# A hybrid decoder step on one core: index queries projected first, index scores as two-head row tiles between the gated pieces, convolution taps in three stages

## The reference

```python
z = einsum('btd,de->bte', rms_norm(x), w_in)
q, k, v, gate_a, qi, ki, wi, glu_a, glu_b, gate_c = split(z)
u = glu_a * sigmoid(glu_b)
# index scores, 8 heads of 64
s = einsum('thd,ld->thl', qi, ki) * 64**-0.5
score = einsum('th,thl->tl', wi * 8**-0.5, relu(s))        # causal
idx = top_k(score, 256)
attn = softmax(q.k[idx] * 64**-0.5 + rel_bias) . v[idx]    # q and k are RMS-normed by head
# convolution branch
c = silu(layer_norm(causal_depthwise_conv(u, width 31) + dw_b))
y = x + concat(attn * silu(gate_a), c * silu(gate_c)) @ w_out
```

## Time and profile before

| | us |
|---|---|
| median of 3 runs (1035.41 to 1056.24) | 1039.91 |
| profiled execution | 1040.58 |
| its span, first to last instruction | 1038.8 |
| PE busy | 930.8 (90%) |
| DVE busy | 694.0 (67%) |
| ACT busy | 372.5 (36%) |
| POOL busy | 85.4 (8%) |

### The profile page before, as it was taken

How to read it: one execution, slowest core, us unless ns; L and a number is a source line. 1 busy time by engine, 2 the same in 40 slices (tenths; PEclk the granted TensorE clock), 3 DMA queues, 4 the chain that set the end, 5 groups by cost and what they waited for, 6 DMA issues and landing times.

```text
span 1038.8 us, 11317 instructions
## 1 busy us (share of the span) xinstructions
PE 930.8 (90%) x3900; PEld 514.4 (50%) x3900; DVE 694.0 (67%) x1598; ACT 372.5 (36%) x830; POOL 85.4 (8%) x90
## 2 busy tenths in 40 slices
PE   3999999936899999999998899697598789999998
PEld 2866666713243444666643334353366555445432
DVE  5309987999896765888878889966487565432111
ACT  6310101102666656889700000122765364221000
POOL 0211010000541000000000000001011101310000
PEclk9999999877999999999999899788699789999999
DMA  8363020200662302001030000005012102320211
GB/s 291 108 188 62 1 81 3 83 0 1 203 210 83 112 34 84 26 22 61 0 102 21 21 20 12 0 1 210 21 52 61 31 11 62 104 100 31 71 62 42
DMA packets 35314, 69.82 MB, mean 67 GB/s; under 512 B 9609, under 2 KB 11953, under 8 KB 35249
## 3 DMA queue, kind: packets, MB, share of 16 engines
q1 hardware_dynamic: 28089, 43.93, 13.0%
q0 software_dynamic: 7168, 25.17, 7.4%
HBM read 58.46 MB, written 11.11 MB: 67 GB/s over the span
## 4 chain that ended last, share of the span: by engine, by line
PE 72%; DVE 21%; ACT 3%; issue 3%; DMA 1%; SPq 1%; DVEq 0%; ACTq 0%
PE ps L491 67%; DVE ctmp L1267 8%; PE ps L494 4%; DVE ct L1241 1%; DMA xn<-in_x_prompt 1%; DVE pv L1469 1%; ACT PTs L942 1%; ACT uT L1120 1%; DVE LB L1470 1%; DVE mcum L1395 0%; DVE zN L1493 0%; ACT relu L1058 0%; DVE pv L1435 0%; DVE uT L1675 0%; ACT sqj L955 0%
## 5 line engine op out<-in xcount | busy, mean ns | idle before, releaser
L491 PE MATMUL ps<-xT,W 128*128 128x344 f32 x960 | 283.8, 458 | 0.0
L491 PEld LDWEIGHTS ps<-xT,W 128*128 128x128 f32 x960 | 184.0, 193 | 97.6 <-issue 5.6
L491 PE MATMUL ps<-W,xT 128*128 128x512 f32 (+3 forms) x576 | 214.7, 531 | 1.2 <-ACT relu L1058 1.2
L1267 DVE SCALAR_TENSOR_TENSOR ctmp<-uT,chw,ctmp 128x1024 f32<-128x1024 f32 x116 | 152.0, 1310 | 4.1
L491 PEld LDWEIGHTS ps<-W,xT 128*128 128x128 f32 (+1 forms) x576 | 94.9, 185 | 113.7 <-issue 113.3
L1088 ACT ACTIVATE sgj<-SC,candn 128x1024 bf16<-128x1024 f32 (+3 forms) x128 | 114.5, 897 | 8.8 <-DVE candn L1373 6.6
L942 ACT ACTIVATE PTs<-ps 128x512 f32<-128x512 f32 (+3 forms) x96 | 43.1, 484 | 125.7 <-PE ps L494 125.7
L1706 DVE TENSOR_TENSOR ps<-ps,TP 128x256 f32<-128x256 f32 (+1 forms) x64 | 26.4, 412 | 71.2 <-PE ps L491 70.8
L1133 ACT ACTIVATE nsq<-ps 128x512 f32<-128x512 f32 (+1 forms) x18 | 10.7, 596 | 164.5 <-DVE nss L1482 120.9
L491 PE MATMUL ps<-kiT,qz 128*128 128x512 f32 (+3 forms) x160 | 61.7, 530 | 7.6 <-ACT relu L1058 6.5
L494 PE MATMUL ps<-Cc,Pm 128*128 128x128 f32 x288 | 46.6, 303 | 17.7 <-ACT PTs L942 17.5
(11 more groups left out here) (308 smaller groups left out, 1046.4 us busy)
## 6 DMA issues: line engine op xcount, KB each, us to landing
W<-in_w_in SPq DMA_DIRECT2D x8, 2048.0 KB, 8.7
xn<-in_x_prompt SPq DMA_DIRECT2D x8, 512.0 KB, 8.2
W<-in_w_out SPq DMA_DIRECT2D x1, 4096.0 KB, 13.3
resid<-in_x_prompt SPq DMA_DIRECT2D x16, 256.0 KB
out<-resid SPq DMA_DIRECT2D x16, 256.0 KB
out<-V SPq DMA_DIRECT2D x8, 256.0 KB
out<-zN SPq DMA_DIRECT2D x8, 256.0 KB, 2.0
bias_rows<-tprow SPq DMA_DIRECT2D x1, 1536.0 KB
```

Source lines behind the costliest of these rows:

```text
L491: return nc.tensor.matmul(out, lhsT, rhs, start=start, stop=stop)
L1267: ins = vec.scalar_tensor_tensor(conv[:, c, :] if j == CW - 1 else acc_, src, chw[:, c, j:j + 1], acc_, ALU.mult, ALU.add)
```

## The change

The order of slices becomes kw, qi, glub, glua, v, and so on. So the index queries exist before the gated slices, and the index scores (steps of a new table `CHUNKS`: block, pair of heads, up to 512 keys; 40 chunks) are set between the 24 pieces of glub and glua. `qz` goes: the two heads of a pair lie in rows 0 to 63 and 64 to 127 of `qiT`, and are multiplied as two matmuls of 64 rows each, into two banks. Relu and weighted add are done per head and chunk, 80 of each where there were 48. The decode rounds 0 and 1 stand in the qi pieces, 2 to 7 behind every second gated piece. VectorE multiplies glua (read from PSUM) into `uT` (`gated`), and not GpSimd. The gated pieces use two banks, b0 and b1, and not four.

The 124 taps are split: 42 between the gated pieces (`TAPS_IN`), 38 more before the search (`TAPS_EARLY` = 80), 44 in the norm stage, a ninth behind each of norms 0 to 8. `ctmp` takes the place of `TP`, so that `TP` is loaded when all taps are done. ScalarE takes 7 pieces of v out before the search. PE waits for VectorE's `decode_u` before the first piece of v.

```diff
-ORDER = ["kw", "glub", "glua", "qi", "v", "ga", "gc", "k", "q"]
+ORDER = ["kw", "qi", "glub", "glua", "v", "ga", "gc", "k", "q"]
-    ctmp = sb("ctmp", [P, 2, SEQ], F32, rGC)
+    ctmp = sb("ctmp", [P, 2, SEQ], F32, rTP)
-    INDEX_STEPS = [(i, h) for i in range(2, NT) for h in range(H)]
+    CHUNKS = [(i, hp, a) for i in range(2, NT) for hp in range(H // 2) for a in range(0, (i + 1) * P, 512)]
...
+    GLU = [(g, m) for c in range(4) for g in ("glub", "glua") for m in range(3 * c, 3 * c + 3)]
+    CACHED_SLOT = [2 * n - 3 for n in range(8)]
...
+    TAPS_IN = [0] * 6 + [1] * 6 + [3] * 12
+    TAPS_EARLY = 80
+    EVACUATED_EARLY = 7
...
-        return min(len(DURING_SEARCH), (r + 1) * 33 // 32)
+        return min(len(DURING_SEARCH), EVACUATED_EARLY + r + 1)
...
 # PE
+        def index_scores(n):
+
+            i, hp, a = CHUNKS[n]
...
+            for e in range(2):
+                begin(("ix", n, e), f"b{2 + 2 * (n % 2) + e}")
+            for e in range(2):
+                r = slice(64 * e, 64 * e + 64)
+                mm(pt(("ix", n, e))[:, 0:width(n)], qiT[r, hp, i * P:(i + 1) * P], kiT[r, a:a + width(n)]).then_inc(plan.fill_sem(("ix", n, e)), 1)
...
+            if j >= 10:
+                cached(j - 10)
+
+        for s, (g, m) in enumerate(GLU):
+            transposed(g, m, 2)
+            for n in chunks_in(s):
+                index_scores(n)
+            if s in CACHED_SLOT:
+                cached(CACHED_SLOT.index(s))
+            if s % 6 == 1 and s > 6:
+                last_rows(s // 6 - 1)
+        last_rows(3)
+        wait(made["decode_u"], 1)
...
-            mm(o[:, a:b], qz[:, h % 2, n // 2 % 2, :], kiT[:, a:b])
...
 # ScalarE
+        for s, (g, m) in enumerate(GLU):
+            a, n = piece_rows(m)
+            if g == "glub":
+                piece_out("glub", m, uT[:, m // 3, CW - 1 + a:CW - 1 + a + n], sT[:, 0], ACT.Sigmoid)
+            for n in chunks_in(s):
+                index_relu(n)
...
 # VectorE
-        taps(0, CW + 24)
...
-        taps(NTAP - 12, NTAP)
...
+        def gated(m):
...
+            vec.tensor_tensor(d, z[:, 0:n], d, ALU.mult).then_inc(plan.drain_sem(("zt", "glua", m)), 1)
...
+        for s, (g, m) in enumerate(GLU):
+            if g == "glua":
+                gated(m)
+            for n in chunks_in(s):
+                weighted(n)
+            if s + 1 in CACHED_SLOT:
+                cached_turn(CACHED_SLOT.index(s + 1))
+            taps(sum(TAPS_IN[:s]), sum(TAPS_IN[:s + 1]))
+        v.wait_ge(made["decode_u_rows"], 4)
+        vec.memset(dsc[:, 7:8], 0.0).then_inc(made["decode_u"], 1)
+        taps(sum(TAPS_IN), TAPS_EARLY)
...
+        rest = NTAP - TAPS_EARLY
         for n in range(len(NORMED)):
             norm(n)
+            if n < 9:
+                taps(TAPS_EARLY + n * rest // 9, TAPS_EARLY + (n + 1) * rest // 9)
...
 # GpSimd
-            pool.tensor_tensor(d, d, glua_r[:, m % 2, 0:n], ALU.mult).then_inc(u_done, 1)
...
 # SP
-        sp.wait_ge(tp_out, 16)
-        sp.dma_start(TP[:], bass.AP(tpd.tensor, P - 1, [[FW - 1, P], [P * FW, H], [1, BAND]])).then_inc(tp_in, 16)
...
+        sp.wait_ge(taps_done, NTAP)
+        sp.wait_ge(tp_out, 16)
+        sp.dma_start(TP[:], bass.AP(tpd.tensor, P - 1, [[FW - 1, P], [P * FW, H], [1, BAND]])).then_inc(tp_in, 16)
```

More of the change, by code:

```diff
@@ L570, in last_rows @@
         def last_rows(c):
[L571 to L581, removed]
+            for m in range(3 * c, 3 * c + 3):
+                wait(*plan.drained(("zt", "glua", m)))
+            o = begin(("cp", c), "b7")
+            tr(o[0:CW - 1, 0:P], uT[:, c, SEQ:SEQ + CW - 1]).then_inc(plan.fill_sem(("cp", c)), 1)
         def index_operands():
@@ L643, in cached @@
                 weigh(7)
[L646 to L658, removed]
+        def index_scores(n):
+            i, hp, a = CHUNKS[n]
+            for m in range(PIECES):
+                wait(*plan.drained(("zt", "qi", m)))
+            for t in range(i + 1):
+                wait(*plan.drained(("kt", t)))
+            for e in range(2):
[3 more added lines that the diff above has]
+                mm(pt(("ix", n, e))[:, 0:width(n)], qiT[r, hp, i * P:(i + 1) * P], kiT[r, a:a + width(n)]).then_inc(plan.fill_sem(("ix", n, e)), 1)
+        for j, m in enumerate(QI_PIECES):
+            transposed("qi", m)
+            if j == 4:
+                back_to_rows("qi")
+            if j == 6:
+                index_operands()
+            if j == 9:
+                own_score()
+            if j >= 10:
[10 more added lines that the diff above has]
+        wait(made["decode_u"], 1)
+        o = begin("urow", "b7")
+        for c in range(4):
+            last = tr(o[0:NB, c * P:(c + 1) * P], sT[:, 1, c, :])
+        last.then_inc(plan.fill_sem("urow"), 1)
         for t in range(NT + 1):
@@ new lines, in index_relu, with last_rows_out @@
+        def index_relu(n):
+            for e in range(2):
+                tag = ("ix", n, e)
+                u = 2 * n + e
+                act.wait_ge(*plan.full(tag))
+                if u >= 4:
+                    act.wait_ge(relu_used, u - 3)
+                nc.scalar.activation(relu[:, u % 4, 0:width(n)], pt(tag)[:, 0:width(n)], ACT.Relu, scale=HD ** -0.5).then_inc(plan.drain_sem(tag), 1)
+        def last_rows_out(c):
+            copy(ulast[:, c * P:(c + 1) * P], pt(("cp", c))[0:CW - 1, 0:P], ("cp", c))
@@ L1253, in taps @@
                 if j == 0:
-                    v.wait_ge(u_done, 3 * c + 3)
+                    for k in range(3 * c, 3 * c + 3):
+                        v.wait_ge(*plan.drained(("zt", "glua", k)))
                 src = uT[:, c, j:j + SEQ]
@@ L1261, in taps @@
                     if j == CW - 1:
-                        if c < 3:
-                            v.wait_ge(last_rows_read, c + 1)
-                        else:
-                            v.wait_ge(*plan.full("cp"))
+                        v.wait_ge(*plan.full(("cp", c)))
                     ins = vec.scalar_tensor_tensor(conv[:, c, :] if j == CW - 1 else acc_, src, chw[:, c, j:j + 1], acc_, ALU.mult, ALU.add)
                 ins.then_inc(taps_done, 1)
-        taps(0, CW + 24)
-        for g in ("glub", "glua"):
-            v.wait_ge(*plan.drained(("zt", g, PIECES - 1)))
-        vec.tensor_tensor(sT[:, 1], sT[:, 1], sT[:, 0], ALU.mult).then_inc(made["decode_u"], 1)
-        taps(CW + 24, NTAP - 12)
         v.wait_ge(*plan.full("Qb"))
@@ new lines, in weighted @@
+        def weighted(n):
+            i, hp, a = CHUNKS[n]
+            for e in range(2):
+                u, h = 2 * n + e, 2 * hp + e
+                src, dst = relu[:, u % 4, 0:width(n)], sc(i)[:, a:a + width(n)]
+                v.wait_ge(*plan.drained(("ix", n, e)))
+                if h == 0:
+                    vec.tensor_scalar(dst, src, wI[:, i, 0:1], None, ALU.mult).then_inc(relu_used, 1)
+                else:
+                    v.wait_ge(relu_used, u)
+                    vec.scalar_tensor_tensor(dst, src, wI[:, i, h:h + 1], dst, ALU.mult, ALU.add).then_inc(relu_used, 1)
@@ L1758, in loaded @@
                 g.wait_ge(cin_in[k], 16 * n)
-        load_cached(0)
-        load_cached(1)
-        loaded(2)
-        for m in range(PIECES):
-            a, n = piece_rows(m)
-            g.wait_ge(*plan.drained(("zt", "glua", m)))
-            g.wait_ge(*plan.drained(("zt", "glub", m)))
-            d = uT[:, m // 3, CW - 1 + a:CW - 1 + a + n]
-            pool.tensor_tensor(d, d, glua_r[:, m % 2, 0:n], ALU.mult).then_inc(u_done, 1)
-        g.wait_ge(u_done, PIECES)
-        for n in range(2, 8):
+        for n in range(8):
             load_cached(n)
@@ L1777, in _ @@
         for i in range(2, NT):
-            g.wait_ge(relu_used, (i - 1) * H)
+            g.wait_ge(relu_used, 2 * sum(1 for x in CHUNKS if x[0] <= i))
             d = sc(i)[:, i * P:(i + 1) * P]
```

150 lines of the change are left out of this document (51 added, 99 removed).

## The result

The changed kernel takes 1079.03 us (median of 4 runs, 1070.96 to 1081.42), and the kernel before 1037.66 on the same chip: a ratio of 1.040, 95% interval 1.033 to 1.046. The profiled execution took 1081.31 us, its span is 1079.2. PE is busy for 926.4 us of it and VectorE for 699.3, against 930.8 and 694.0: the work is nearly the same, and it is the waiting that has grown.

The account below looks back on a forecast made before the run. PE had 72% of the chain, but VectorE was taken to set norm 9: 516.9 + 113.6 + 58.1 + 2 = 690.6, plus a 377.4 us tail, span 1068.0, time 1069.8, said as 1070; range 1046 to 1092.

Parts of the forecast that it names:

- qi pieces: Index queries, now first, from 48.66 us: 55.6 + 6.4 + 4.9 us on PE, gated pieces start at 115.6.
- A chunk: Index scores on PE: a pair of 64-row, 512-column matmuls overlaps and takes 1.00 us.
- Rival C: Index scores: the matmul pairs do not overlap, each 1.72 us and not 1.00; 1093 us, chance 0.06.
- First half: Gated pieces 0 to 11: PE bounds with 90.2 us against VectorE's 64, plus 3; piece 12 at 209.
- Second half: Gated pieces 12 to 23: VectorE bounds with 78.5 us against PE's 74.0; v starts at 295.3.
- Rival A: Gated pieces 12 to 23: VectorE's work slips into earlier idle time, PE's 74.0 us counts; 1060 us, chance 0.22.
- The search: Behind 38 taps: starts at 346.5, free rounds of 4.58 us, round 25 waits for PE's pieces, dC at 516.9.
- Norm stage: From dC to norm 9, VectorE bounds: 113.6 us, 58.1 for 44 taps, 2 for waits; norm 9 at 690.6.
- Rival B: Between dC and norm 9: PE bounds, the 44 taps lie in VectorE's idle time; 1012 us, chance 0.08.
- Half clock: Between dC and norm 9: PE might stay at 1.2 GHz, 174 us of work against 173.7 available.
- rival D: Between dC and norm 9: PE at 1.2 GHz throughout just hidden, +10 us counted; 1080 us, chance 0.09.
- Tail: Everything behind norm 9: keeps its 377.4 us, PE busy for 340.66.

Follow-up runs that it names:

- the twelve moved taps: Changed kernel with 12 more taps in gated slots 6 to 11 and 12 fewer in the norm stage: 1063.76 us, ratio 1.017.

## Why the prediction was right

Forecast: 1070 us, slower, at 0.70. Measured: 1079, slower, inside the range of 1046 to 1092. On the clock of the span the forecast was 1068.0 and 1079.2 came. Point by point:

- **qi pieces.** Gated piece 0 was to start at 115.6 and starts at 118.2. The terms were there, and one was too small: the three pieces behind the 128 small products of `srow` took 15.8 us and not 3 x 4.63 = 13.9, at a granted clock of 0.63 in their first 4.7 us. The trace of the kernel before had it too, and I had not looked: the clock was 0.52 from 199 to 204 us. The rows, before and after:

```profile
199.46 16.30 PE L491 MATMUL ps<-xT,W 128*128 128x344 f32 x48
87.92 15.83 PE L498 MATMUL ps<-xT,W 128*128 128x344 f32 x48
```

  The other 0.7 us are PE's opening product, which the forecast left out.
- **A chunk.** Four matmuls in 1.99 us, so a pair in 1.00, as the row it was priced by. Rival C falls by the row at 281.39.
- **First half.** 96.0 us against 93.4, with 3.3 of named waits, where I had allowed 3. The rest is in PE's busy time (92.71 against 90.2): a piece with other products on both sides takes 4.83 us from start to start (276.56 to 281.39, for one), and not the 4.63 of an unbroken row of six.
- **Second half.** 84.2 against 86.3. VectorE was the bound, as said, and its taps took 1.28 and not 1.32. PE waited 6.8 us for it at the end. Rival A falls here: VectorE did not slip its work into the 38 us that it had idle in the first half. That they were there, the twelve moved taps show.
- **The search** started at 347.9, forecast 346.5; 47 us more on PE gave VectorE nothing there, as predicted, since its taps end at 347.9; without the 38 taps the seven pieces held it just as long. `dC` ended at 522.0, forecast 516.9. The 24.2 us from the last round to the end of `dC` and the pace of the rounds (4.59) are exact. Of the 5.1 us, 3.1 were there when VectorE gave `decode_u` free, and 1.7 came in v, which took 63.87 us and not 62.13, its first 11.6 at a granted clock of 0.80, behind PE's wait of 6.8.
- **Norm stage.** 175.2 us against 173.7. Two errors nearly cancel. Without the taps it takes 119.4 (the run without the late ones) and not 113.6 + 2: I took VectorE's 12.6 us of waits at L1410 and L1435 away and put 2 back, while 6.0 of them stay. The taps take 55.8 and not 58.1. Rival B needed more than 58 us of waits in the old stage; it falls by the same run.
- **Half clock.** The granted clock in the norm stage was 0.76, after 0.64 in the stretch before it, so PE does spend part of it at 1.2 GHz. The Trainium skill ("TensorE: Matmul & The Clock Gate", section "Why this matters for your kernels") warns of this, and these rows agree. But PE waits for VectorE there in any case. Without the taps the clock is 0.87 and the stage 55.8 us shorter, no more than the taps are long: rival D's price was not paid.
- **Tail.** 382.1 against 377.4. The same instructions took 372.7 to 382.1 us in the kernels of this study (377.8, 380.2, 374.0 are some). PE was busy for 336.89 to 343.85 us of it, at a granted clock of 0.94 to 0.92. I had taken the tail as fixed, and it scatters by 9. That is the largest single part of what the forecast missed.

So the misses were 2.6 and 2.6 up to piece 12, -2.1 in the second half, 2.0 in the search, 1.4 in the norm stage and 4.7 in the tail, 11.2 together. Those of PE have one sign, since I priced its pieces by an unbroken row at full clock. That the total is 9 us off and no more owes something to luck: the second half and the price of a tap were too high, all else too low. The step that decided, 44 taps into a stage where VectorE was the bound, was right, and right in size. So was the other half of it, that PE's gain does not reach VectorE, which starts the search when it did before, with 44 taps fewer done.

## What to carry to other kernels

Find the stretch in which the second engine has no waits, and count what the change puts there: PE was 72% of the chain, and yet between the search and norm 9 each 1.28 us on VectorE cost 1.28 us. Time won for one engine is worth only what the next common point lets through; here the search let 13 of 47 us through. A split such as `TAPS_IN` is filled by idle time: 18 taps fit the first half where 6 were put. And ask of a new order what the second engine needs first: here the input of the taps moved back, and VectorE stood idle at the start.

## What the runs showed of the hardware

I had not expected that VectorE and GpSimd would slow each other this much. A multiply-add of 128x1024 with two operands in SBUF took 1283 ns alone and 2184 in the mean beside GpSimd's products and sums; GpSimd's went from 2.85 to 3.66 us and from 2.36 to 2.78. Even a `COPY` of 32 columns went from 181 to 629 ns, while the counts of 768 columns, with one operand, stayed at 1012. The Trainium skill ("SBUF — State Buffer", section "Who interferes with whom") says that a VectorE instruction with two SBUF inputs contends with a GpSimd instruction that reads SBUF, and one with a single input outside the two-port modes does not. The taps and the counts agree. The same section lists `copy` among the operations that can enter a two-port mode, which would fit its growth; which mode it ran in, no row tells. For the two-port modes it says that the one that comes second stands still until the other is done. Single taps took from 1.28 to 3.26 us, and some `COPY`s 181 ns and others 2.2 us; so one instruction can lose some 2 us and the next nothing. Small operations are hit unevenly: `tk<-cnt,sgn` has two inputs too and stayed at 166 ns where `cnt<-acnt,halfn` grew. Whether an instruction waits at its start or shares in the middle, these rows don't tell.
